# Transposes for the spreads of deviations, a widened reciprocal for the head norms, and first-attention values made by features

## What is computed

```python
def rms_norm(x, g):                      # eight such norms over 1024 features
    y = xf * lax.rsqrt(jnp.mean(xf * xf, axis=-1, keepdims=True) + EPS)
    return (y * g).astype(x.dtype)

def even_mixer(xn, xcn, w_in, ...):      # the first attention: 8 heads, 2 key/value heads of 64
    ...
    v = proj[..., Q_END + KV_WIDTH:].reshape(B, S, N_KV_HEADS, HEAD_DIM)   # values, of x and of the context

def nsa_mixer(q, k_c, v_c, k_s, v_s, k_w, v_w, ...):
    q = (rmsnorm(q.reshape(B, S, NSA_HEADS, d), q_norm) * (d ** -0.5))     # one norm for each head of 64
    ... rmsnorm(kv(k_s), kn_slc) ... rmsnorm(kv(k_w), kn_win)
```

## Time and profile before

| | |
|---|---|
| three runs | 1206.35, 1212.85, 1214.12 us |
| median | 1212.85 us |
| span of the profiled execution | 1207.4 us |
| TensorE busy | 1149.0 us, 95% |
| VectorE busy | 814.4 us, 67% |
| ScalarE busy | 589.9 us, 49% |
| GpSimd busy | 81.8 us, 7% |

### The profile page before, as it was taken

How to read it: one execution, slowest core, us unless ns; L and a number is a source line. 1 busy time by engine, 2 the same in 40 slices (tenths; PEclk the granted TensorE clock), 3 DMA queues, 4 the chain that set the end, 5 groups by cost and what they waited for, 6 DMA issues and landing times.

```text
span 1207.4 us, 24317 instructions
## 1 busy us (share of the span) xinstructions
PE 1149.0 (95%) x10429; PEld 1092.4 (90%) x10429; DVE 814.4 (67%) x1490; ACT 589.9 (49%) x1084; POOL 81.8 (7%) x100
## 2 busy tenths in 40 slices
PE   5888789999998999999989999999999999999999
PEld 2687689999997999999989888888999999999999
DVE  3783668898886767555674678787664665877543
ACT  2434556454544545454465557653234445655432
POOL 0000110000011000001100111112600001000000
PEclk9789999999999999999998999999999999999999
DMA  9751548889884555751653232232123464855520
GB/s 388 291 207 60 215 170 329 334 340 349 320 328 174 222 222 223 255 187 43 246 175 105 106 105 80 97 105 71 38 72 106 157 211 159 323 198 185 208 84 14
DMA packets 32363, 226.41 MB, mean 188 GB/s; under 512 B 3584, under 2 KB 4736, under 8 KB 5120
## 3 DMA queue, kind: packets, MB, share of 16 engines
q1 hardware_dynamic: 30528, 221.20, 49.1%
q10 hardware_dynamic: 1728, 3.67, 0.8%
HBM read 223.80 MB, written 1.05 MB: 186 GB/s over the span
## 4 chain that ended last, share of the span: by engine, by line
PE 86%; DVE 8%; ACT 4%; DMA 1%; issue 1%; POOL 0%; SPq 0%; DVEq 0%; POOLq 0%
PE bank L562 23%; PE bank L563 22%; PE bank L564 22%; PE bank L1041 2%; PE bank L687 2%; DVE sb_tmp L1915 1%; DVE sb_ring L1930 1%; DVE sb_wlo L1889 1%; PE bank L580 1%; PE bank L1032 1%; PE bank L1063 1%; DMA sb_ring<-in_ada 1%; PE bank L590 1%; PE bank L600 1%; PE bank L1229 1%; PE bank L1247 1%
## 5 line engine op out<-in xcount | busy, mean ns | idle before, releaser
L562 PE MATMUL bank<-sb_xh,sb_whi 128*128 128x256 f32 x1488 | 422.9, 284 | 9.0 <-DVE sb_wlo L1889 6.7
L563 PE MATMUL bank<-sb_xl,sb_whi 128*128 128x256 f32 x1488 | 414.3, 278 | 0.0
L564 PE MATMUL bank<-sb_xh,sb_wlo 128*128 128x256 f32 x1488 | 414.3, 278 | 0.0
L1889 DVE TENSOR_TENSOR sb_wlo<-sb_ring,sb_whi 128x1024 fp32r<-128x1024 f32 (+1 forms) x197 | 239.1, 1220 | 138.5 <-ACT sb_whi L1375 138.1
L562 PEld LDWEIGHTS bank<-sb_xh,sb_whi 128*128 128x128 f32 x1488 | 281.6, 189 | 17.6 <-issue 12.8
L563 PEld LDWEIGHTS bank<-sb_xl,sb_whi 128*128 128x128 f32 x1488 | 282.2, 190 | 0.1
L564 PEld LDWEIGHTS bank<-sb_xh,sb_wlo 128*128 128x128 f32 x1488 | 281.7, 189 | 0.0
L1375 ACT ACTIVATE sb_whi<-sb_ring 128x1024 fp32r<-128x1024 f32 (+1 forms) x197 | 206.7, 1053 | 88.7 <-PE bank L564 81.3
L1889 DVE TENSOR_TENSOR sb_wlo<-sb_more,sb_whi 128x1024 fp32r<-128x1024 f32 x108 | 131.0, 1222 | 64.8 <-ACT sb_whi L1375 64.8
L562 PE MATMUL bank<-sb_hh,sb_whi 128*128 128x256 f32 x608 | 168.4, 277 | 0.0
L564 PE MATMUL bank<-sb_hh,sb_wlo 128*128 128x256 f32 x608 | 167.8, 276 | 0.0
(11 more groups left out here) (378 smaller groups left out, 1845.6 us busy)
## 6 DMA issues: line engine op xcount, KB each, us to landing
sb_more<-in_w SPq DMA_DIRECT2D x34, 1024.0 KB, 6.7
sb_ring<-in_w SPq DMA_DIRECT2D x32, 1024.0 KB, 6.0
sb_ring<-in_adaT SPq DMA_DIRECT2D x26, 1024.0 KB, 7.6
sb_ring<-in_f SPq DMA_DIRECT2D x22, 1024.0 KB, 5.0
sb_more<-in_adaT SPq DMA_DIRECT2D x18, 1024.0 KB, 9.5
sb_ring<-in_gn SPq DMA_DIRECT2D x8, 1024.0 KB, 4.9
sb_ring<-in_gd SPq DMA_DIRECT2D x8, 1024.0 KB, 4.9
sb_ring<-in_up SPq DMA_DIRECT2D x8, 1024.0 KB, 5.9
```

Source lines behind the costliest of these rows:

```text
L562: te.matmul(out, wh, rh, start=start, stop=False, skip_group_check=skip)
L563: te.matmul(out, wh, rl, start=False, stop=False, skip_group_check=skip)
L564: return te.matmul(out, wl, rh, start=False, stop=stop, skip_group_check=skip)
L1889: ve.tensor_tensor(lo, x, hi.bitcast(F32), ALU.subtract).then_inc(*lo_dve.up(n))
```

## The change

It has three parts.

1. At lines 642 and 1311 `te.matmul` becomes `te.transpose`, on the same operands.
2. For the head norms the reciprocal no longer works in place on 8 columns: its input is read with each column repeated 64 times, and it writes 512 columns into `wide`, which are the first two of VectorE's three tiles of `tmp`. Four transposes of 128 of these columns take the place of the eight matmuls. The reciprocal also waits for the transposes of the pair before, and ScalarE's root waits for the reciprocal and no longer for TensorE.
3. The values of the first attention are made like all other products, the weight stationary and 256 tokens moving (48 matmuls for x and the context), copied to `tmp` by ScalarE, turned by 4 transposes, and copied to `v0`. The turning stands behind the first `scores0`.

```diff
+        wide = flat(tmp[:, 3:5, :]).rearrange("p (t c d) -> p t c d", t=2, c=4)
...
-                    end = te.matmul(ps[:, t * 128:(t + 1) * 128], columns(dev[:, NORMS.index(norm) if slot is None else slot, t:t + 1]), ident, start=True, stop=True)
+                    end = te.transpose(ps[:, t * 128:(t + 1) * 128], columns(dev[:, NORMS.index(norm) if slot is None else slot, t:t + 1]), ident)
...
-            _, hi, lo = unit_of(u)
-            P.wait_ge(*lo_done(u))
             for e, (rh, rl) in enumerate(((xh, xl), (xch, xcl))):
+                ps = take(RG, ("vf", e), (act, ("vf", e)))
+                product(u, rh, rl, ("mix0", "ctx")[e], ps[:, 0:T]).then_inc(*pe.up(("vf", e), ("unit", u)) if e else pe.up(("vf", e)))
+
+            def values_turned(e):
+                ps = take(RG, ("v", e), (act, ("v", e)))
+                P.wait_ge(*act.at("vf", e))
                 for t in range(2):
-                    ps = take(RG, ("v", e, t), (act, ("v", e, t)))
-                    q = slice(t * 128, (t + 1) * 128)
-                    for k in range(KT):
-                        c = slice(k * 128, (k + 1) * 128)
-                        end = mm3(ps[:, 0:128], rh[:, k, q], rl[:, k, q], hi[:, c], lo[:, c], k == 0, k == KT - 1)
...
+                    end = te.transpose(ps[:, t * 128:(t + 1) * 128], ta_of(("vf", e))[:, t * 128:(t + 1) * 128], ident)
+                end.then_inc(*pe.up(("v", e)))
...
-                        for u, p in enumerate(HALVES):
-                            c = 2 * e + u
-                            end = te.matmul(ps[p, o:o + 128], columns(hdev[:, j // 2 % 2, t, c:c + 1], 64), ident, start=True, stop=True)
+                        pair = wide[:, t, 2 * e:2 * e + 2, :].rearrange("p c d -> p (c d)")
+                        end = te.transpose(ps[:, o:o + 128], pair, ident)
...
-                        end = te.matmul(ps[:, o:o + 128], columns(odev[:, t, 2 * p2 + e:2 * p2 + e + 1]), ident, start=True, stop=True)
+                        end = te.transpose(ps[:, o:o + 128], columns(odev[:, t, 2 * p2 + e:2 * p2 + e + 1]), ident)
...
-                    A.wait_ge(*pe.at("v", e, t))
-                    sc.activation(v0[:, e, t, :], ps_of(("v", e, t))[:, 0:128], ACT.Copy).then_inc(*act.up(("v", e, t)))
+                A.wait_ge(*pe.at("vf", e))
+                sc.activation(temp(("vf", e), (pe, ("v", e))), ps_of(("vf", e))[:, 0:T], ACT.Copy).then_inc(*act.up(("vf", e)))
+            for e in range(2):
+                A.wait_ge(*pe.at("v", e))
+                sc.activation(v0[:, e, :, :], ps_of(("v", e))[:, 0:T].rearrange("p (t c) -> p t c", t=2), ACT.Copy).then_inc(*act.up(("v", e)))
...
-                d = flat(hdev[:, j // 2 % 2, :, :])
+                d = hdev[:, j // 2 % 2, :, :]
                 V.wait_ge(*act.at("hsd", j))
-                ve.reciprocal(d, d).then_inc(*dve.up(("hrs", j)))
+                if j > 1:
+                    V.wait_ge(*pe.at("hb", j - 2))
+                ve.reciprocal(wide, d.unsqueeze(3).to_broadcast([128, 2, 4, 64])).then_inc(*dve.up(("hrs", j)))
```

More of the change, by code:

```diff
@@ L735, in tensor_program @@
             u, _ = F.take("mixin")
-            _, hi, lo = unit_of(u)
-            P.wait_ge(*lo_done(u))
             for e, (rh, rl) in enumerate(((xh, xl), (xch, xcl))):
-                for t in range(2):
-                    ps = take(RG, ("v", e, t), (act, ("v", e, t)))
-                    q = slice(t * 128, (t + 1) * 128)
-                    for k in range(KT):
-                        c = slice(k * 128, (k + 1) * 128)
-                        end = mm3(ps[:, 0:128], rh[:, k, q], rl[:, k, q], hi[:, c], lo[:, c], k == 0, k == KT - 1)
-                    end.then_inc(*pe.up(("v", e, t), ("unit", u)) if (e, t) == (1, 1) else pe.up(("v", e, t)))
-            F.done(u)
+                ps = take(RG, ("vf", e), (act, ("vf", e)))
[3 more added lines that the diff above has]
+                P.wait_ge(*act.at("vf", e))
+                for t in range(2):
+                    end = te.transpose(ps[:, t * 128:(t + 1) * 128], ta_of(("vf", e))[:, t * 128:(t + 1) * 128], ident)
+                end.then_inc(*pe.up(("v", e)))
             def scores0(i):
@@ L776, in values0 @@
                 P.wait_ge(*act.at("pt", i, 1))
-                P.wait_ge(*act.at("v", 1, 1))
+                P.wait_ge(*act.at("v", 1))
                 for k in range(4):
@@ L806, in tensor_program @@
                     scores0(i)
+                if i == 0:
+                    for e in range(2):
+                        values_turned(e)
                 if 0 <= i - 2 < N0:
@@ L1607, in f1_deviation @@
                 if j > 3:
-                    A.wait_ge(*pe.at("hb", j - 4))
+                    A.wait_ge(*dve.at("hrs", j - 4))
                 sc.activation(flat(hdev[:, j // 2 % 2, :, :]), ps_of(("hs", j))[:, 0:8], ACT.Sqrt, bias=C("eps"), scale=1.0 / 64).then_inc(*act.up(("hsd", j)))
@@ L2031, in vector_program @@
             ve.tensor_scalar(nsink[:, :], C("sink"), -1.0, None, ALU.mult).then_inc(*dve.up("nsink"))
-            V.wait_ge(*pe.at("v", 1, 1))
+            V.wait_ge(*pe.at("vf", 1))
             V.wait_ge(*dve.at("nsink"))
```

## The result

The changed kernel takes 1224.04 us in the median of six runs (1222.33 to 1227.1), the kernel before 1211.51 beside it. The ratio is 1.0128, with a 95% interval from 1.0108 to 1.0148: 15.5 us slower, by more than 1%. The forecast was 1223 us. The medians lie only 12.5 us apart and the means 13.0 (a ratio of 1.0108, the lower end of the interval), and the twelve times do not show how the given ratio follows from them. So the loss is 12.5 to 15.5 us; where this text sets it against other ratios, it takes the 15.5. The profiled execution went from a span of 1207.4 to 1220.5 us, +13.1.

What follows compares the result with a forecast made beforehand. TensorE, busy 1149.0 of 1207.4 us, was taken as the bound. Values -5.1, spreads -3.2, head norm waits +13.7 and clock +5 gave +10.4 us on the median 1212.85: 1223 us, range 1210 to 1233.

Steps and rivals of the forecast that it cites:

- Values, -5.1: First attention: 48 wide matmuls for 96 narrow ones give 5.5 us back, a later exponential costs 0.4.
- Rival 4: The values' gain is lost again in the loop of the pairs; sum +10.4 + 5.1, 1228 us, chance 0.12.
- Spreads, -3.2: Spreads of norms and odev as transposes: seven times 0.23 gives 1.6 us, four groups of odev 1.6.
- Size of the reciprocal, 3.45 us: VectorE's head norm reciprocal at 512 columns, carried on from the times at 8 and 60 columns.
- Rival 3: The wide reciprocal is cheap, under 2.4 us; at 0.69 us the sum is -8.3, 1204.5 us, chance 0.08.
- The waits add up, 5 D - 2.5 = +13.7: In f1 each period grows by 2.75 us and delays accumulate; D is how much longer a reciprocal is.
- TensorE's waits near 20 us: Sign in the profile after: TensorE waits near 20 us for the reciprocal in place of 4.7.
- The clock, +5: In f1 the granted clock falls in three of the longer waits, 1.7 us each; bounds 0 and +13.
- rival 2: The clock falls in nearly every wait; sum +13.7 + 13 - 8.3 = +18.4, 1231 us, chance 0.18.
- Rival 1: The waits are as long as worked out but the clock holds; sum +5.4, 1218 us, chance 0.25.
- The sum: Whole kernel: -5.1 - 3.2 + 13.7 + 5 = +10.4 us, put on the median 1212.85, giving 1223 us.
- slower by over 1%: Outcome for the whole kernel, over 12 us slower, given chance 0.40; within 1% had 0.54.

Runs made afterwards that it cites:

- e7_filler: Changed kernel plus eight unread identity matmuls in each of the first four waits for the head norms' reciprocal; ratio to before 1.0070.
- e5_small_then_wide: Changed kernel with the head norms' reciprocal on 8 columns, then spread over 512 by a multiplication by 1.0; ratio to before 0.9933.
- the two experiments: e4, 8.2 us faster than the kernel before, and e3, 23.9 us slower than it.
- e4: Changed kernel with its head norms as before, both other parts kept; ratio to before 0.9932, 8.2 us faster.
- e6: Changed kernel with the 512-column reciprocal made twice in a row; ratio to before 1.0300, 36.3 us slower.
- e9: Changed kernel with the 8 columns first copied out to 512, then the reciprocal of the stored numbers; one run, 1233.09 us.
- e11: Changed kernel with the reciprocal made twice and unread matmuls in the waits, sixteen in the first four, eight in the fifth; ratio to before 1.0255.
- e3: Kernel before with only the head norms changed to the widened reciprocal and transposes; ratio to before 1.0198, 23.9 us slower.
- e8: Kernel before with an extra, unread 512-column reciprocal ahead of each 8-column one; ratio to before 1.0199, 24.1 us slower.
- e2: Kernel before with only the spreads of norms' and output deviations made as transposes; ratio to before 0.9958, 5.1 us faster.
- e10: Changed kernel with head norms as before, plus eleven unread matmuls ahead of the fifth product of queries; ratio to before 0.9960.
- e12: Changed kernel with head norms as before, plus eleven unread matmuls ahead of the product of the fourth f unit; ratio to before 0.9947.
- e1: Kernel before with only the values of the first attention made by features and turned; ratio to before 0.9959, 5.0 us faster.

## Why the prediction was right, and where it was off

- **Values, -5.1.** Shown: -5.0 alone (2.4 to 7.4 us), 5.2 up to the first scores and 4.6 kept in the trace. Rival 4 (the gain does not arrive) is out.
- **Spreads, -3.2.** A spread fell to 0.21 as said, a group of odev to 0.36 where 0.41 was said. There are eight spreads and not nine, so the term should have been 6 x 0.23 + 1.6 = -3.0. Alone -5.1 (2.8 to 7.4); 3.1 by the corrected count.
- **Size of the reciprocal, 3.45 us.** 3.345: the line through 8 and 60 columns holds to 512 within 3%. (3345 - 195) / 504 is 6.25 ns a column. The Trainium skill's repeat count of 8 (VectorE: DVE Perf Modes, First, the fixed hardware budget) gave an estimate of 4.3, too long by 29%. Rival 3 (cheap) is out.
- **The waits add up, 5 D - 2.5 = +13.7.** This is the step that carried the forecast. With D = 3.15 as measured it says +13.3. In e7_filler the stage is 15.1 longer than before, with 1.9 more lost to the clock: 13.2 if all of that counts. The periods there at full clock, longer by 2.4 to 2.8 us each, show the step itself: 3.15 - 0.5 = 2.65 was its number. So the waits add up from pair to pair.
- **TensorE's waits near 20 us.** 17.1 + 0.5 at the spreads, and 2.5 at the second scores, 20.1. But "3.3 to 6 us six times" was wrong, and did not fit the forecast's own 20: four waits are of 3.6 to 4.95 us, the fifth of 0.5, the sixth of 2.5.
- **The clock, +5: the term that was mis-sized.** The stage is 23.1 longer, 13.2 of it by waits, so the clock costs 9.9 us. The rows of TensorE agree: the same matmuls kept it busy for 83.3 us here and for 73.5 in e5_small_then_wide. The step that failed is "I take three falls in the longer waits". The waits of 3.6 us have slow transposes behind them just as those of 4.9 (the timeline above), and what is slow then is the chain that leads to the next reciprocal. All four periods are slower than in e7_filler, by 1.4 to 2.8 us, 2.1 in the mean, where three of 1.7 were said. It lies nearer to rival 2's +13 than to my +5. Rival 1 (the clock holds) is out.
- **The sum.** -8.3 + 13.7 + 5 = +10.4 was said; -8.2 + 23.9 = +15.7 is the sum of the two experiments, and 15.5 the whole by the given ratio. That the median came within 1.04 us of the forecast owes something to luck: it stood on a median of before that is 1.34 us higher than the new one, and the two new medians lie 3 us closer than their ratio. The sum of +10.4 stayed just under the 12 us of a whole per cent; with the clock's term at 9.9 it would have been +15.3, and "slower by over 1%" the likeliest outcome and not, with 0.40 against 0.54, the second.

The -7.2 us ahead of f1 in the profiled pair must not be read as the gain. Versions with the same program up to there entered f1 at 591.2 to 600.1 us (the changed kernel, e4, e5, e6, e7, e9 and e11), and at 599.4 to 605.5 (before, e3 and e8). The means, 596.4 and 601.9, lie 5.5 us apart, which is about what the values and the first spreads were to give; a single pair could have shown anything from -1 to 14.

## What to carry to other kernels

Before work is moved from TensorE to the engine that feeds it, ask whether that engine's result is waited for: here 0.5 us saved a pair was paid with 3.15 us in a loop that returns to itself five times, so the price was five times the delay, with the clock on top, and no stage behind won it back. Take an expensive function of the few numbers, and spread the result by a cheap pass (0.62 us in place of 3.35), or leave the spreading to the matmul. A wait costs TensorE twice, by its length and by the clock behind it; of the second, filling the waits with idle matmuls gave back 8.0 of the 23.1 us, but the bank that they write and its last reader must be free too.

## Of the hardware, not expected

- The length of a wait does not tell whether the clock falls. The output products of the first attention waited 3.12 us before as after the earlier trace rows. Before, the clock stood at 1.00; now matmuls start 0.21 us apart in place of 0.12. Timeline of TensorE in the changed kernel:

```profile
150.03 0.58 PE L564 MATMUL bank<-sb_ah,sb_whi 128*128 128x256 f32 x1 [3.12 <-DVE sb_wlo L1894]
150.41 0.42 PE L565 MATMUL bank<-sb_al,sb_whi 128*128 128x256 f32 x1
150.62 0.41 PE L566 MATMUL bank<-sb_ah,sb_wlo 128*128 128x256 f32 x1
```

  And the stretch there, the clock third from the end:

```profile
150.00:156.00 6.00, 5.97 (x28) 5.98 (x29) 3.75 (x4) 2.37 (x3) 0.00 (x0) 0.51 1.02 412
```

  The prediction used that very row as evidence that a wait of 3.12 us leaves the clock alone. It was one draw: all fourteen traces have this wait (3.12 or 3.13 us), with TensorE busy for 5.20 of the 6 us ahead of it at clock 1.00. In the 6 us behind it the clock was 1.00 in seven (before, e2, e6, e7, e8, e10, e12), 0.50 or 0.51 in five (the changed kernel, e1, e3, e4, e11) and 0.72 in two (e5, e9). Both outcomes occur with and without the change of the values.
- A reciprocal on VectorE costs 6.25 ns a column between 8 and 512 columns of fp32 (195 and 3345 ns), one number read 64 times or 512 stored ones (3353 ns); a multiplication of 512 columns costs 0.43 us.
- Four transposes of 128x128 between products took 0.36 us up to the next product's start in e2_spreads (L1311), 0.09 each, and 0.41 in the earlier trace rows.
